# A square root of a dummy column behind the squares of each norm, in a two-model kernel on one core

## What is computed

```python
def rmsnorm(x, g):
    xf = x.astype(jnp.float32)
    y = xf * lax.rsqrt(jnp.mean(xf * xf, axis=-1, keepdims=True) + EPS)
    return (y * g.astype(jnp.float32)).astype(x.dtype)
```

## Time and profile before

| | us |
|---|---|
| median of three executions | 3246.74 |
| lowest, highest | 3244.81, 3247.67 |
| the profiled execution's own time | 3242.28 |
| its span, first to last instruction | 3240.4 |
| busy: TensorE matmul | 2631.2 (81% of the span) |
| busy: VectorE | 2218.0 (68%) |
| busy: ScalarE | 1019.2 (31%) |
| busy: GpSimd | 738.4 (23%) |
| DMA | 976.51 MB, 301 GB/s on the mean |
| mean granted TensorE clock | 0.91 |

### The profile page before, as it was taken

One profiled execution on the slowest core, in us unless ns is written; L12 is line 12 of the kernel. 1 busy time (PEld: TensorE's weight loads), 2 busy tenths in 40 slices (PEclk: granted clock), 3 DMA queues, 4 the chain that ended last, 5 costly groups with the idle time before them and its releaser, 6 DMA issues.

```text
span 3240.4 us, 37121 instructions
## 1 busy us (share of the span) xinstructions
PE 2631.2 (81%) x13830; PEld 1983.2 (61%) x13830; DVE 2218.0 (68%) x3855; ACT 1019.2 (31%) x2144; POOL 738.4 (23%) x679
## 2 busy tenths in 40 slices
PE   8999998897699989689874688768876778775666
PEld 5999986686589989689764445225542446321122
DVE  3886866737537868758616666986679775987755
ACT  3433322112233343333322342233322343221222
POOL 0000000003200000000000233443434433445543
PEclk9999998999899999899887889889888889887799
DMA  7766942240058859549545799999999999999998
GB/s 285 267 236 264 366 177 95 94 143 25 20 200 325 357 207 355 196 171 356 220 148 225 318 406 420 421 421 412 421 420 420 396 409 419 421 421 420 419 422 335
DMA packets 136868, 976.51 MB, mean 301 GB/s; under 512 B 15501, under 2 KB 15509, under 8 KB 18976
## 3 DMA queue, kind: packets, MB, share of 16 engines
q0 software_dynamic: 90512, 656.51, 49.8%
q1 hardware_dynamic: 45072, 312.26, 25.3%
q10 hardware_dynamic: 1152, 6.04, 0.5%
HBM read 973.69 MB, written 1.06 MB: 301 GB/s over the span
## 4 chain that ended last, share of the span: by engine, by line
PE 48%; DMA 27%; DVE 15%; ACT 5%; issue 5%; POOL 1%; DVEq 0%; ACTq 0%; POOLq 0%
PE psum L610 48%; DMA rows<-in_peer,eidx 26%; DVE arena L1424 2%; DVE yacc L1427 2%; DVE arena L1560 1%; DVE wlow L1424 1%; DVE rows L2111 1%; PE psum L613 1%; ACT L1046 1%; DVE arena L1430 1%; DVE arena L1427 1%; ACT u L1046 1%; DMA wring<-in_keys 1%; POOL rows L2238 0%; ACT dots L1046 0%
## 5 line engine op out<-in xcount | busy, mean ns | idle before, releaser
L610 PE MATMUL psum<-rows,diag 128*128 128x512 f32 x1392 | 784.1, 706 | 390.8 <-ACT diag L1046 384.3
L2111 DVE CUSTOM_DVE_ANT_0 rows<-rows,h2tok 128x1024 f32<-128x1024 f32 x512 | 626.1, 1225 | 367.4 <-DMA rows<-in_peer,eidx 360.0
L2238 POOL DMA_INDIRECT rows<-in_peer,eidx x512 | 624.7, 1220 | 975.4 <-PE psum L610 556.5
L610 PEld LDWEIGHTS psum<-rows,diag 128*128 128x128 f32 x1392 | 285.1, 218 | 817.6 <-ACT diag L1046 539.7
L610 PE MATMUL psum<-u_hi,whigh 128*128 128x256 f32 x1760 | 504.3, 287 | 17.7 <-DVE u_lo L1427 14.1
L610 PE MATMUL psum<-u_lo,whigh 128*128 128x256 f32 x1760 | 501.0, 285 | 0.0
L610 PE MATMUL psum<-u_hi,wlow 128*128 128x256 f32 x1760 | 500.8, 285 | 0.0
L1424 DVE TENSOR_TENSOR wlow<-wring,whigh 128x2048 fp32r<-128x2048 f32 x165 | 376.9, 2288 | 161.3 <-ACT whigh L1046 155.1
L1046 ACT ACTIVATE whigh<-wring 128x2048 fp32r<-128x2048 f32 x165 | 314.0, 1908 | 206.8 <-PE psum L610 133.8
L610 PEld LDWEIGHTS psum<-u_hi,whigh 128*128 128x128 f32 x1760 | 340.5, 193 | 21.2 <-issue 15.0
L610 PEld LDWEIGHTS psum<-u_lo,whigh 128*128 128x128 f32 x1760 | 341.1, 194 | 0.0
(11 more groups left out here) (265 smaller groups left out, 3234.3 us busy)
## 6 DMA issues: line engine op xcount, KB each, us to landing
arena<-in_ada_t POOLq DMA_DIRECT2D x112, 1024.0 KB, 7.0
wring<-in_ffn_w_gate SPq DMA_DIRECT2D x55, 1024.0 KB, 6.0
wring<-in_ffn_w_up SPq DMA_DIRECT2D x55, 1024.0 KB, 6.4
wring<-in_ffn_w_down SPq DMA_DIRECT2D x55, 1024.0 KB, 6.5
wring<-in_w_in SPq DMA_DIRECT2D x32, 1024.0 KB, 9.1
wring<-in_peer_wq SPq DMA_DIRECT2D x32, 1024.0 KB, 9.1
wring<-in_ssd_w_in SPq DMA_DIRECT2D x30, 1024.0 KB, 4.8
wring<-in_w_out SPq DMA_DIRECT2D x16, 1024.0 KB, 9.1
```

Source lines behind the costliest of these rows:

```text
L610: return nc.tensor.matmul(out, lhsT, rhs, start=start, stop=stop, skip_group_check=shared)
L2111: v.tensor_tensor_reduce(out=rows[:, n % SLOTS, 0:D], in0=rows[:, n % SLOTS, 0:D], in1=h2tok[:, t, :], scale=1.0, scalar=0.0, op0=ALU.mult ...
L2238: pool.indirect_dma_start(out=rows[:, n % SLOTS, :], out_offset=None, in_=A[f"peer{u // 2}"], in_offset=bass.IndirectOffsetOnAxis(ap=eidx[ ...
```

## The change

A tile `warm` of one column is added behind `eps`, and a function that takes the square root of the column `eps` into it. Nothing reads `warm`. It is called at the head of `deviation`, that is behind the squares of each of the nine norms and ahead of the waits for their sums; behind the square of the grouped norm; and in `mix(0, 0)` behind the copy of the transposed probabilities, ahead of the squares of `ostat`. It is executed eleven times.

```diff
         eps = sb("eps", [P, 1])
+        warm = sb("warm", [P, 1])
...
+            def warm_sqrt():
+
+                f(warm[:], eps[:, 0:1], ACT.Sqrt)
+
             def deviation(n):
+                warm_sqrt()
                 if n:
...
             f(z[:], xbc[:, 0:XB, :], ACT.Square).then_inc(gsq_ready, 1)
+            warm_sqrt()
             act.wait_ge(gms_ready, 1)
...
                   psum[:, 0:4, :].rearrange("p a (b s) -> p (a b) s", b=2)[:, :, lo:T], ACT.Identity).then_inc(probT_ready, 1)
+                if g == 0:
+                    warm_sqrt()
                 yield 31
```

## The result

Ten executions of each kernel: the changed one takes 3238.65 us on the median (3233.77 to 3243.49), the one before 3245.68 us (3242.79 to 3247.67). The ratio is 0.9977, with a 95% interval from 0.9968 to 0.9985: 0.23% faster, 7.0 us by the medians, and 4.9 to 10.4 us by the interval. The forecast was 3238.1 us.

What follows compares the result with a forecast made beforehand. The prediction took the chain of waits, with six exposed table loads in it, as the bound. Direct gains of 6.40 + 1.27 = 7.67 us and 1.0 for the clock gave 3246.74 - 8.7 = 3238.1 us; range 3232.5 to 3243.0.

Steps and rivals of the forecast that it cites:

- The six loads: Exposed table loads at norms 2, 3, 5, 6, the last and `ostat` move ahead of waits: 5 x 1.28 plus 1.27 us.
- The direct sum of 7.67 us: Gain from roots starting earlier: 6.40 us at five norms plus 1.27 us at `ostat`, before any clock effect.
- The rival that a part doesn't arrive: One or two of six terms missing, no clock gain: 3240.3 to 3241.6 us; chance 0.22.
- the 1.89 us of GpSimd: Issue before a DMA behind the last norm, taken to move along; if released otherwise, up to 1.28 us lost.
- The dummies: Unread roots of 0.20 us each; the five at norms 0, 1, 4, 7 and the grouped norm cost nothing.
- cover: ScalarE's 1.96 us wait at norms 2, 6 and the last fits load and dummy, 0.4 us to spare.
- TensorE's clock: Shorter pauses at norm 5 and the last may delay or avoid clock falls: +1.0 us, ends -3.3 and +6.6.
- The price of a load: 1.28 us by the rows, not the skill's 2.66; rival of a dearer load: 3231.4 us, chance 0.02.
- The layout: Rival: new tile shifts later tiles by 32 bytes, slowing the gathers; 3242.9 to 3256.7 us; chance 0.07.

Runs made afterwards that it cites:

- e3: Changed kernel with dummy roots only at norms 2, 3, 5, 6, the last and the unit that runs alone: ratio 0.9971, 3239.57 us.
- e2: Changed kernel with the dummy column inside the 32 bytes eps already has, so no tile moves: ratio 0.9964 to the kernel before, 3237.36 us.
- e4: Kernel before with four alternating exponential and root dummies between sums and root at norms 2, 3, 5, 6 and the last: ratio 1.0061.
- e9: Changed kernel measured again, unaltered, against the kernel before: ratio 0.9976, 3239.88 us against 3247.63.
- e11: Kernel before with 16, 16, 9, 12, 9 constant matmuls filling TensorE's pauses behind norms' sums: ratio 0.9979, 3241.05 us.
- e1: Kernel before with only the unused one-column tile added, moving later tiles by 32 bytes: ratio 0.9999, 3248.83 us against 3247.98.
- e6: Changed kernel with 24, 24, 16, 16, 16 constant matmuls behind the sums of norms 2, 3, 4, 5, 7: ratio 0.9982, 3242.76 us.
- e8: Kernel before, no dummy roots, with 29, 29, 16, 21, 16 constant matmuls in TensorE's pauses: ratio 1.0024, 3255.64 us.
- e12: Changed kernel with an exponential ahead of the scan's loop and constant matmuls in more of TensorE's pauses: ratio 0.9932, 3226.48 us.

## Why the prediction was right

**The six loads.** Each step came as worked out: no load more, each behind its squares or behind the copy that ends ScalarE's work there, the root 0.03 to 0.09 us behind what it waits for. The direct sum of 7.67 us lies beside 7.0 and 7.8 measured, and beside 8.4 and 10.6 by the medians in e3 and e2, which move the same six loads. The prediction's reading of the page was loose in one point: the 1% of "ACT L1046" is all 24 loads in the chain, and the six that it moves are a quarter of that. e4 shows from the other side that time between the sums and the root reaches the end. The rival that a part doesn't arrive, which stood on the 1.89 us of GpSimd behind the last norm, has no support: that step kept its length and moved with the root, and on the mean of several profiles (e9) the first gather comes 8.7 us earlier, no less than the sum.

**The dummies.** 198 ns against the 0.20 taken, and 0.46 us of cover left where 0.4 was forecast. That the five without a load cost nothing agrees with e3, without being resolved.

**TensorE's clock** was the weak term. The +1.0 us stood on the hope that a pause cut from 5.5 to 4.2 us, or from 4.7 to 3.4, would spare a fall of the clock. Both falls came anyway in the profile after. Behind norm 5 the clock fell in the profiles of e3 and e9 as well, in e9 for 6.8 us as before, in e3 for 3.4 us. How long it stays down differs from profile to profile, and no run here ties that to the shorter pause. What the clock is worth came out only where the pause was filled: 6.6 us in e11, with a mean granted clock of 0.917 and not 0.911. The changed kernel's mean clock is that of the kernel before to within 0.001, which by the rate of e11 is 1 us at most, give or take 2: no run shows the term, and its sign isn't known. The number nearest to the measured change is the direct sum without this term.

**The price of a load.** The figure of about 2.66 us for a switch in the Trainium skill ("ScalarE: Activation LUTs", What ACT_TABLE_LOAD costs) isn't borne out: e4 has four switches in a row at 1.50 us each, a dummy root or exponential of 0.20 us included, and in the changed kernel a load starts 0.01 us behind a square over 128x512 elements (440.80 to 440.81).

**The layout**, the rival on the slower side, is shut out by e1 to within 3 us and by e2.

**The starting point.** The forecast was made from a median of three, 3246.74 us; with ten it is 3245.68. That shift of 1.1 us and the clock term of 1.0 cancel in the comparison of 3238.1 with 3238.65, so the closeness of these two numbers is partly luck. The measured change is 7.0 (or 7.8) against a forecast of 8.7.

## What to carry to other kernels

Where an engine waits for another's result and then has to load a table, take the function once on a dummy ahead of the wait, behind the last work with the old set; what counts is whether the load stands in the chain of waits, since the six moved here, of 66, were worth 7.7 us by their rows and e4 bears that price out. Look for such loads through the whole chain: 16 more stand in it here in the stage of the gathers, untried. Compare the spacing with and without the load (here 1.36 and 0.08 us at two norms) before believing any figure for it. When a pause of TensorE is unavoidable, look at what the clock does behind it: cutting a pause from 5.5 to 4.2 us didn't keep the clock up, filling it did, and filling it past its end gave the gain back (e6, e8).

## What I had not expected

An fp32 matmul of 128x256 appears as two records of 0.22 us spacing, so 24 of them took 10.5 us where I had counted 6. And the clock's falls are worth more than the six loads: e12 gains 21 to 22 us, of which the roots and the exponential account for 7.67 + 1.28 = 9 by their rows, and the rest, 12 to 13 us, is left for the fills. That rest is a difference and not a measurement of its own; the one run with fills alone, e11, shows 6.6 us for five of the ten. It is less than all the table loads in the chain, 29.4 us, of which 16 were left where they are.
